# Turning activation rows for the MLP and gate stages with VectorE's 32x32 blocks and a way through memory, instead of with TensorE transposes

## The reference, cut to what matters

```
h = x + nsa_mixer(rms_norm(x, norm_mix_g), ...)            # attention, 2048 -> 2048
u = rms_norm(h, norm_mlp_g)
h = h + square(relu(u @ mlp_w1)) @ mlp_w2                  # 2048 -> 8192 -> 2048
u = rms_norm(h, ple_norm_g)
out = h + sigmoid(u @ ple_w_gate) * (p @ ple_w_proj)       # 2048 -> 2048, 256 -> 2048
```

## Time and profile before

| | |
|---|---|
| median of 3 runs | 1243.33 us (1242.25 to 1243.96) |
| the profiled execution, its time | 1243.53 us |
| its span (first to last recorded instruction) | 1241.8 us |
| PE busy | 1231.8 us (99%) |
| PEld busy | 1019.3 us (82%) |
| DVE busy | 700.6 us (56%) |
| ACT busy | 571.5 us (46%) |
| POOL busy | 57.5 us (5%) |
| main DMA queue, share of 16 engines | 56.3% |

### The profile page before, as it was taken

How to read it: one execution, slowest core, us unless ns; L and a number is a source line. 1 busy time by engine, 2 the same in 40 slices (tenths; PEclk the granted TensorE clock), 3 DMA queues, 4 the chain that set the end, 5 groups by cost and what they waited for, 6 DMA issues and landing times.

```text
span 1241.8 us, 16004 instructions
## 1 busy us (share of the span) xinstructions
PE 1231.8 (99%) x5831; PEld 1019.3 (82%) x5831; DVE 700.6 (56%) x966; ACT 571.5 (46%) x784; POOL 57.5 (5%) x57
## 2 busy tenths in 40 slices
PE   8999999999999999999999999999999999999998
PEld 7888788888888888888878888888888888888886
DVE  5676546887765645554445454454545445555654
ACT  7554433554445544433444443444433445445543
POOL 0001000000000001000010000000000001000000
PEclk9999999999999999999999999999999999999999
DMA  9767664333335665556655556665556665555551
GB/s 335 205 191 210 200 173 138 116 104 103 102 119 187 183 193 182 188 194 196 193 168 194 189 191 194 184 188 190 189 191 193 186 191 184 182 192 174 203 195 63
DMA packets 123741, 222.07 MB, mean 179 GB/s; under 512 B 8996, under 2 KB 18584, under 8 KB 123672
## 3 DMA queue, kind: packets, MB, share of 16 engines
q1 hardware_dynamic: 123128, 220.55, 56.3%
q10 hardware_dynamic: 544, 0.52, 0.2%
HBM read 218.95 MB, written 2.10 MB: 178 GB/s over the span
## 4 chain that ended last, share of the span: by engine, by line
PE 97%; DVE 1%; POOL 1%; DMA 0%; issue 0%; ACT 0%; ACTq 0%
PE acc L1112 87%; PE tr L1165 2%; PE sc L1232 1%; POOL rs L395 1%; PE sc L1245 1%; PE sc L1231 1%; DVE w_lo L728 0%; PE tr L1154 0%; PE sc L1154 0%; PE acc L1139 0%; PE tr L1283 0%; PE tr L1279 0%; PE tr L1280 0%; DMA h<-in_x_dram 0%; PE tr L1259 0%; PE tr L1264 0%
## 5 line engine op out<-in xcount | busy, mean ns | idle before, releaser
L728 DVE TENSOR_TENSOR w_lo<-w_raw,w_hi 128x1024 fp32r<-128x1024 f32 x412 | 507.9, 1239 | 440.4 <-ACT w_hi L447 437.4
L447 ACT ACTIVATE w_hi<-w_raw 128x1024 fp32r<-128x1024 f32 x412 | 434.2, 1059 | 436.7 <-PE acc L1112 431.5
L1112 PE MATMUL acc<-w_hi,a_hi 128*128 128x512 f32 x958 | 383.1, 400 | 2.2 <-issue 1.5
L1112 PE MATMUL acc<-w_hi,a_lo 128*128 128x512 f32 x958 | 373.4, 390 | 0.0
L1112 PE MATMUL acc<-w_lo,a_hi 128*128 128x512 f32 x958 | 373.0, 389 | 0.0
L1112 PE MATMUL acc<-w_hi,b_hi 128*128 128x512 f32 x640 | 254.4, 398 | 0.0
L1112 PE MATMUL acc<-w_hi,b_lo 128*128 128x512 f32 x640 | 249.3, 390 | 0.0
L1112 PE MATMUL acc<-w_lo,b_hi 128*128 128x512 f32 x640 | 249.0, 389 | 0.0
L1112 PEld LDWEIGHTS acc<-w_hi,a_hi 128*128 128x128 f32 x958 | 180.1, 188 | 42.7 <-issue 3.8
L1112 PEld LDWEIGHTS acc<-w_lo,a_hi 128*128 128x128 f32 x958 | 180.1, 188 | 37.8 <-issue 2.4
L1112 PEld LDWEIGHTS acc<-w_hi,a_lo 128*128 128x128 f32 x958 | 179.8, 188 | 38.1
(11 more groups left out here) (171 smaller groups left out, 611.8 us busy)
## 6 DMA issues: line engine op xcount, KB each, us to landing
w_raw<-in_mlp_w_dram SPq DMA_DIRECT2D x256, 512.0 KB, 3.7
w_raw<-in_nsa_w_in_dram SPq DMA_DIRECT2D x79, 512.0 KB, 3.8
w_raw<-in_nsa_w_out_dram SPq DMA_DIRECT2D x32, 512.0 KB, 3.7
w_raw<-in_ple_w_gate_dram SPq DMA_DIRECT2D x32, 512.0 KB, 4.0
w_raw<-in_nsa_cmp_w_dram SPq DMA_DIRECT2D x8, 512.0 KB, 4.8
w_raw<-in_ple_w_proj_dram SPq DMA_DIRECT2D x4, 512.0 KB, 4.1
out_dram<-h SPq DMA_DIRECT2D x7, 256.0 KB, 4.3
h<-in_x_dram SPq DMA_DIRECT2D x3, 512.0 KB, 8.5
```

Source lines behind the costliest of these rows:

```text
L447: nc.scalar.activation(w_hi[:, u % SPLIT, 0:width], w_raw[:, u % RAW, 0:width], ACT.Copy).then_inc(hi_done, 1)
L728: nc.vector.tensor_tensor(w_lo[:, u % SPLIT, 0:width], w_raw[:, u % RAW, 0:width], f32(w_hi[:, u % SPLIT, 0:width]), ALU.subtract).then_in ...
L1112: last = nc.tensor.matmul(acc[c % 2][t][:], xs[:, kt, toks], ws[:, u % SPLIT, m * NW:(m + 1) * NW], start=(kt == 0 and n == 0), stop=(kt = ...
```

## The change

The 24 sets of PE transposes are gone. In place of a set:

- **DVE** turns the 32x32 blocks of the 128 x 1024 values within each quadrant of 32 partitions, in two instructions of 128 x 512, from `h` or `stage` into `blocks`, which is the old buffer `junk` (`turn_blocks`).
- **SP** issues four DMAs of 32 partitions each, 128 KB, to a tensor in device memory (`turn_away`: per DMA 128 runs of 1 KB), and, once these have landed, two DMAs of 256 KB back into `turned`, which is the old buffer `q_t` (`turn_back`: per DMA 512 runs of 512 bytes). They stand between two weight loads, on the same queue; the table beside each chunk's loads gives the unit after which each goes. Since they differ by chunk, SP's loop over the quarters now has eight chunks written out.
- **ACT** writes the `hi` part from `turned` (`turned_gain`, four instructions, or `turned_hidden`, one of 128 x 1024) behind its split of unit k = 6 or 7, and **DVE** the `lo` part behind unit k = 7.
- **PE** waits for `turned_split` before units of the chunks that use the values (`turned_by`).

Cut to its core:

```diff
+        blocks = junk[:]
+        turned = q_t[:].rearrange("p j s -> p (j s)")
...
+            def turn_away(n, i=0):
+
+                sp.wait_ge(blocks_turned, TT * (n + 1 + 4 * i))
+                if n < T_HID and n > 0:
+                    sp.wait_ge(turn_in, 16 * TT * n)
+                for a in range(P // QUAD):
+                    sp.dma_start(turn_dram[:, :, a].rearrange("b i t f -> i b (t f)"),
+                                 blocks[a * QUAD:(a + 1) * QUAD].rearrange("i (b f) -> i b f", b=P // QUAD))\
+                      .then_inc(turn_out, 16)
+
+            def turn_back(n, i=0):
+
+                sp.wait_ge(turn_out, 16 * (P // QUAD) * (n + 1 + 4 * i))
+                if n < T_HID and n > 0:
+                    sp.wait_ge(turned_split, n)
+                for t in range(TT):
+                    sp.dma_start(turned[:, t * NW:(t + 1) * NW].rearrange("p (a f) -> p a f", a=P // QUAD),
+                                 turn_dram[:, :, :, t].rearrange("b i a f -> (b i) a f")).then_inc(turn_in, 16)
...
+            def up_turn(j):
+
+                return ((T_HID + j, 4, 5),)
...
+            def turned_hidden(j, i):
+
+                act.wait_ge(turn_in, 16 * TT * (T_HID + j + 1 + 4 * i))
+                nc.scalar.activation(b_hi[:, 4 * j:4 * j + 4].rearrange("p m (g j) -> p m g j", j=QUAD),
+                                     turned.rearrange("p (g m j) -> p m g j", m=NW // P, j=QUAD),
+                                     ACT.Copy).then_inc(turned_hi, 1)
...
@@ scalar: hidden chunks @@
-                        if k == 4:
-                            transposed_hi(R_MLP + j - 1, b_hi, 4 * (j - 1), None, i)
+                        if k == 7:
+                            turned_hidden(j - 1, i)
...
@@ vector @@
+            def turn_blocks(n, src, i=0):
+
+                if not (isinstance(i, int) and n == 0):
+                    dve.wait_ge(turn_out, 16 * (P // QUAD) * (n + 4 * i))
+                for t in range(TT):
+                    nc.vector.transpose(
+                        blocks.rearrange("p (b t m j) -> p t m b j", b=P // QUAD, t=TT, j=QUAD)[:, t],
+                        src(t).rearrange("p (m b i) -> p m b i", b=P // QUAD, i=QUAD)).then_inc(blocks_turned, 1)
...
@@ vector: hidden chunks @@
                         if k == 4:
-                            transposed_lo(R_MLP + j - 1, b_hi, b_lo, 4 * (j - 1), None, i)
+                            dve.wait_ge(squared, TT * j + 4 * TT * i)
+                            turn_blocks(T_HID + j - 1, lambda t: stage[:, t], i)
+                        if k == 7:
+                            turned_hidden(j - 1, i)
...
@@ vector: C_MLP, its last extra work @@
                 if k == 2:
                     add_to_h(C_OUT + 3, 3)
+                    dve.wait_ge(acc_read[(C_OUT + 3) % 2][TT - 1], (C_OUT + 3) // 2 + 1)
+                    turn_blocks(T_H1 + 3, h_rows(3))
...
-                if k == 4:
-                    transposed_lo(R_H1 + 3, a_hi, a_lo, 12, GAIN_MLP)
+                if k == 7:
+                    turned_gain(T_H1 + 3, a_hi, a_lo, 12, GAIN_MLP)
...
@@ tensor @@
+            def turned_by(n, k, i=0):
+
+                pe.wait_ge(turned_split, n + k // 2 + 1 + 4 * i)
...
                     for k in range(UPC):
-                        if k == 2:
-                            pe.wait_ge(squared, TT * j + 4 * TT * i)
-                            transpose_set(R_MLP + j - 1, from_stage, i)
                         if j == 4:
-                            split_by(R_MLP, k, i)
+                            turned_by(T_HID, k, i)
```

More of the change, by code:

```diff
@@ L343, in _, with up_chunk @@
                     load(u, w_out[:, UNIT_KT * k:UNIT_KT * (k + 1), n * NW:(n + 1) * NW], slot(u))
+                    if n == 3:
+                        turn_steps(k, ((T_H1, 2, 3), (T_H1 + 1, 5, 7)))
             w1, w2 = rows(mlp_w1), rows(mlp_w2)
[L345 to L355, removed]
+            def up_chunk(j, i=0, turn=()):
+                for k in range(UPC):
+                    u = FIRST[C_MLP + j] + k
+                    load(u, w1[:, UNIT_KT * k:UNIT_KT * (k + 1), bass.ds(i * D + j // 8 * D + j % 8 * NW, NW)], slot(u), i * (8 * UPC))
+                    turn_steps(k, turn, i)
@@ new lines, in down_chunk, with down_turn @@
+            def down_chunk(j, i, turn=()):
+                for k in range(UPC):
+                    u = FIRST[C_MLP + j] + k
+                    load(u, w2[:, bass.ds(i * KT + UNIT_KT * k, UNIT_KT), bass.ds((j - 4) * NW, NW)], slot(u),
+                         i * (8 * UPC))
+                    turn_steps(k, turn, i)
+            def up_turn(j):
+                return ((T_HID + j, 4, 5),)
+            def down_turn(n):
+                return ((n, 2, 3),)
+            up_chunk(0, 0, ((T_H1 + 2, 2, 4),))
@@ new lines, in _ @@
+            up_chunk(1, 0, ((T_H1 + 3, 2, 3),))
+            with sp.Fori(0, QUARTERS - 1) as q:
+                for j in (2, 3):
+                    up_chunk(j, q, up_turn(j - 2))
+                for j in range(4, 8):
+                    down_chunk(j, q, up_turn(j - 2) if j < 6 else ())
+                for j in (8, 9):
+                    up_chunk(j, q)
+            last_q = QUARTERS - 1
+            for j in (2, 3):
+                up_chunk(j, last_q, up_turn(j - 2))
+            for j in range(4, 8):
+                down_chunk(j, last_q, up_turn(j - 2) if j < 6 else down_turn(T_H2 + j - 6 - 4 * last_q))
@@ L470, in transposed_hi, with turned_gain @@
                     last.then_inc(tr_hi[b], 1)
+            def turned_gain(n, dst_hi, kt0, gain):
+                act.wait_ge(turn_in, 16 * TT * (n + 1))
+                for m in range(NW // P):
+                    last = nc.scalar.activation(tokens(dst_hi[:, kt0 + m]), turned_tile(m), ACT.Copy,
+                                                scale=const_t[:, gain + kt0 + m:gain + kt0 + m + 1])
+                last.then_inc(turned_hi, 1)
+            def turned_hidden(j, i):
[3 more added lines that the diff above has]
+                                     ACT.Copy).then_inc(turned_hi, 1)
             def sum_squares(norm, n):
@@ L746, in transposed_lo, with turned_gain, turned_hidden, h_rows @@
                     last.then_inc(tr_done[b], 1)
+            def turn_blocks(n, src, i=0):
[5 more added lines that the diff above has]
+                        src(t).rearrange("p (m b i) -> p m b i", b=P // QUAD, i=QUAD)).then_inc(blocks_turned, 1)
+            def turned_gain(n, hi, lo, kt0, gain):
+                dve.wait_ge(turned_hi, n + 1)
+                for m in range(NW // P):
+                    kt = kt0 + m
+                    last = nc.vector.scalar_tensor_tensor(
+                        out=tokens(lo[:, kt]), in0=turned_tile(m), scalar=const_t[:, gain + kt:gain + kt + 1],
+                        in1=tokens(f32(hi[:, kt])), op0=ALU.mult, op1=ALU.subtract)
+                last.then_inc(turned_split, 1)
+            def turned_hidden(j, i):
+                dve.wait_ge(turned_hi, T_HID + j + 1 + 4 * i)
+                hi, lo = (x[:, 4 * j:4 * j + 4].rearrange("p m (g j) -> p m g j", j=QUAD) for x in (b_hi, b_lo))
+                nc.vector.tensor_tensor(lo, turned.rearrange("p (g m j) -> p m g j", m=NW // P, j=QUAD), f32(hi),
+                                        ALU.subtract).then_inc(turned_split, 1)
+            def h_rows(n):
+                return lambda t: h[:, t, n * NW:(n + 1) * NW]
             def mean_square(n, norm):
```

90 lines of the change are left out of this document (51 added, 39 removed).

## The result

The change makes the kernel slower where I forecast 16 us faster. In its first eight runs the changed kernel took 1252.97 us in the median (1246.64 to 1257.31), the kernel before 1243.71 us: a ratio of 1.0072, 95% interval 1.0052 to 1.0092. The forecast was 1227.4 us, with 1221 to 1236 as the range. The profiled execution is the quickest of the first eight, 1246.64 us, with a span of 1244.9 us, 3.1 us over the one before; what follows accounts for that one.

What follows compares the result with a forecast made beforehand. PE, busy for 99% of the span, was taken to bound the kernel: 1243.5 - 21.6 (transposes removed) + 4.8 (four late hidden pieces) + 0.7 (C_MLP) = 1227.4 us, range 1221 to 1236.

Steps and rivals of the forecast that it cites:

- The removal, 24 x 0.90 = 21.6 us: On PE: each set of transposes costs 0.90 us, nothing hidden under it, so 24 sets save 21.6 us.
- The blocks, 1.29 us; ACT 1.06, DVE 1.23: Late hidden piece: DVE's pair of block transposes 1.29 us, ACT's copy 1.06, DVE's subtraction 1.23.
- I take 3.7: Late pieces' four DMAs to memory: 3.7 us, a weight load's landing time; bounds 2.8 and 5.8 us.
- The way back, 4.9 us: Late pieces' two DMAs from memory, first issue included: 4.9 us; bounds 4.1 and 5.8 us.
- where I had 0.6: C_MLP: PE waits 0.6 us for the fourth piece of h, 0.7 us with the restart.
- After a gap its second matmul starts 0.33 us behind the first: PE's restart after a wait: 0.33 us instead of 0.23, making a hidden piece's 1.1 us wait cost 1.2 us.
- the things that would make me wrong: Signs against: PE waits for w_lo, waits over 20 us, granted clock falling after a wait, set-free chunk over 21.76 us.
- What costs nothing: Other work of ACT, DVE, SP and the queue: no cost; next chunk's first w_lo has 3.1 us of room.
- rival (3): The round trip through memory bounds the splits, so all 16 hidden pieces cost: 1276 us; chance 0.06.
- The gate's fourth piece, "at nothing": Fourth piece of h before the gate: due 2.72 us later behind a projection unit, so costed at nothing.
- Rival (2): The same waits but longer, steps at their upper ends: PE waits 5.2 us each quarter, 1246 us; chance 0.16.
- The break-even in rival (3), a round trip of 12.6 us: Round trip at which the five late pieces' waits alone would cancel the gain: 8.6 + 4 = 12.6 us.

Runs made afterwards that it cites:

- e_late_pe: The changed kernel with six sets (fourth hidden piece of each quarter, fourth of h before MLP and gate) back on PE: 1229.94 us.
- e_busy: The changed kernel with PE transposes of the identity, computed for nothing, before the late waits of the hidden chunks and C_MLP: 1245.67 us.
- e_busy2: The changed kernel with unused PE transposes of the identity before the late waits of the hidden chunks, C_MLP and the gate stage: 1242.94 us.

## Why the prediction was wrong

- **The removal, 24 x 0.90 = 21.6 us: right.** 0.86 us by doubling, 0.92 us by removing 22 without a wait. PE did bound the kernel, and DVE's 31 us of block transposes were as hidden as I said.
- **The blocks, 1.29 us; ACT 1.06, DVE 1.23: right**, within 0.02 us.
- **"I take 3.7" for the way out: the step that failed first.** It was 5.6 us, and 5.4 to 5.7 in all four quarters. I wrote that a load's 512 KB were in front on the same queue, and then took the time of a single load, as if the four DMAs were alone. The rows had the reason: 1.8 us for the lone output tiles, 8.7 us where the queue was full. The issue of four took 1.4 us to the last instead of 1.0. Without loads in front it was 3.6 us, and the way back 4.2 us instead of the forecast 4.9. With it the four waits for `b_lo` came to 10.2 us, where the sum had 4 x 1.1 = 4.4.
- **The way back, 4.9 us: nearly right in the hidden quarters**, 5.25 us in the chunk shown and 4.0 to 4.6 in the others. In `C_MLP` it was 6.0 us (430.80 to 436.76 in the chain), with one load issued 1.3 us in front of it, and DVE's addition ended 1.6 us later than I had it, counted from the moment at which PE was ready for the piece; so 3.5 us of wait there where I had 0.6.

```profile
430.80 0.52 SPq L327
...
436.76 0.03 ACT a_hi L555
```

- **"After a gap its second matmul starts 0.33 us behind the first": the price of a wait was wrong.** I took it from a gap of 0.21 us, and no row of before had a longer one in this part. A wait of 2 or 3 us cost itself and mostly 1.7 us more by the halved clock. I named the clock among the things that would make me wrong and gave it neither a price nor a rival. The Trainium skill ("TensorE: Matmul & The Clock Gate", the section on how the clock's oscillation bites in real kernels) describes a kernel that waits for its transfers again and again and each time starts again at the low clock; these traces agree in kind (0.57 to 0.73 in the lowest stretch behind each of four waits, in a kernel that else has 1.00), and differ in that not every wait does it and that the clock here fell up to 1.5 us after the matmuls had started again.
- **"What costs nothing": half right.** In the hidden quarters it held: no wait for `w_lo`, so rival (3) didn't come about, though the round trip grew by 2.3 us of its 3.1 us of room. In front of the MLP it failed: ACT stood 5.8 and 6.7 us waiting for `q_t` (to 401.77 and 415.48) with its splits queued behind, and PE waited 1.6 and 0.9 us for `w_lo`. Four pieces share one buffer and follow each other closely there, which is the likely reason but not one that a run shows by itself. I had worked out the cover for a chunk of the hidden quarters and used it for all.
- **The gate's fourth piece, "at nothing": wrong**, 1.4 us. By the steps for `C_MLP` it had 2.1 us to spare (2.72 less 0.6); it came 3.5 us later than that.
- **Rival (2), the same waits but longer, 0.16**, comes nearest, with 1246 us as its upper end, but that it nearly meets the profiled 1246.64 us is luck. It had 24 us of waits and no clock; it was 17.6 us of waits and 6.8 us of clock, in the quickest of the first eight runs, and their median lies 7 us above its upper end. Its sum has a slip as well: by its own steps the term for `C_MLP` is 4.7 us and not 3, 1247.7 in all.
- **The break-even in rival (3), a round trip of 12.6 us**, is summed wrongly too: 21.6 us less the 5.5 that I took leave 16.1, or 3.2 us for each of five places, and 8.6 + 3.2 = 11.8 us. Nothing else in the forecast hangs on it.

The sum had 5.5 us for all waits and their restarts. They came to 17.6 us: 10.2 instead of 4.4 for the hidden pieces, 3.5 instead of 0.6 in `C_MLP`, 1.4 instead of nothing at the gate, 2.5 instead of nothing for `w_lo`. This alone would have given some 1240 us, above the range's 1236. The clock, which no case priced, made 24.4 us of them, and that takes back the whole of the 21.6 us.

## What to carry to other kernels

On an engine that is 99% busy, work moved elsewhere pays only if its result is back before the engine wants it: cost the latest consumer of each moved piece first, with what stands in front of it on the queue, and put the hand-over as early as its input allows (here one unit earlier was worth 13 us). In this kernel a wait of TensorE of 2 us or more cost up to nearly twice its length; where it couldn't be avoided, transposes computed for nothing in its place kept the clock and made the time steady. Where a few of many pieces are late, moving the many and leaving the few (`e_late_pe`) gave 13.3 of 16.2 us.

## What the runs showed of the hardware that I had not expected

- The granted clock of a TensorE that was busy for 99% of a millisecond fell to its 1.2 GHz level 1.5 us after the end of a single wait of 3.3 us, and stayed there for 3 us. In the traces of all versions the clock fell with each of the seven waits of 2.8 us or more behind 360 us, with 11 of the 17 between 1.86 and 2.72 us, and with none that was shorter, leaving aside the last two microseconds of a run; what decides between them isn't settled by these runs.
- 20 to 30 transposes of 128x128, 2.35 to 3.44 us long, where PE would else have waited were enough to keep it at 1.00 at 11 places of 11 (`e_busy`, `e_busy2`).
- A block transpose of 128 x 512 fp32 on VectorE takes 0.66 to 0.72 us (medians 0.684 and 0.688), as long as an addition of that shape (0.685).
- The issue of a DMA on SP took 0.55 us with 512 runs (median of the changed kernel), between the 0.37 us of a load with 256 and the 1.4 us of the slowest issue in the earlier trace rows. With 128 runs it took 0.43 us, more than the load's: the first of the four 0.33 us and the next two 0.43 and 0.48 in the chain shown. So the number of runs isn't all that counts.
